# The norm of the recurrent mixer's memory, moved from the fifth FFN's beginning to the fourth's

## The reference

```python
def rms_norm(x, g):
    y = x * lax.rsqrt(jnp.mean(x * x, axis=-1, keepdims=True) + NORM_EPS)
    return y * g

# first block, second layer
x = ffn_step(x, ...)                               # third FFN
x = x + mx[5] * diff_attention(...)                # its last matrix is w_o
x = ffn_step(x, norm_g[1, 2], ...)                 # fourth FFN ("ffn", 3)
x = rms_norm(x, final_g)                           # final norm of the first block
# second block, first layer
x = x + 0.5 * swiglu_ffn(x, ffn_pre_norm[0], ...)  # fifth FFN ("ffn", 4)
u = rms_norm_2(x, mix_norm[0])
k, v = jnp.split(rms_norm_2(mem, mem_norm_g) @ w_kv, 2, axis=-1)   # memory's keys and values
...                                                # recurrent mixer and memory attention
```

## Time and profile before

| | |
|---|---|
| time, median of 3 runs | 2893.64 us (2890.03 to 2897.38) |
| the profiled execution | 2892.83 us, of which the span is 2891.2 us |
| TensorE's mean granted clock | 0.983 |
| TensorE, matmuls | busy 2770.5 us (96%) |
| VectorE | busy 2065.3 us (71%) |
| ScalarE | busy 1025.5 us (35%) |
| GpSimd | busy 81.5 us (3%) |

### The profile page before, as it was taken

One profiled execution on the slowest core, in us unless ns is written; L12 is line 12 of the kernel. 1 busy time (PEld: TensorE's weight loads), 2 busy tenths in 40 slices (PEclk: granted clock), 3 DMA queues, 4 the chain that ended last, 5 costly groups with the idle time before them and its releaser, 6 DMA issues.

```text
span 2891.2 us, 49358 instructions
## 1 busy us (share of the span) xinstructions
PE 2770.5 (96%) x19380; PEld 2447.1 (85%) x19380; DVE 2065.3 (71%) x3075; ACT 1025.5 (35%) x1158; POOL 81.5 (3%) x152
## 2 busy tenths in 40 slices
PE   6999999999999999999999899998999999998999
PEld 4888878888878888788799899887799989986999
DVE  6877778866777777776666766666767766665677
ACT  5222224222232222233344444452144434343433
POOL 1000000000000000000000000000000000000000
PEclk9999999999999999999999999999999999998999
DMA  8444441443334444322245344421044544443354
GB/s 328 160 147 180 172 154 66 161 151 131 131 117 160 146 181 170 112 95 74 84 175 189 131 174 174 180 88 60 3 166 175 202 125 174 185 164 66 117 186 177
DMA packets 68704, 421.42 MB, mean 146 GB/s; under 512 B 7672, under 2 KB 8824, under 8 KB 26592
## 3 DMA queue, kind: packets, MB, share of 16 engines
q1 hardware_dynamic: 48032, 341.26, 31.8%
q0 software_dynamic: 20576, 78.78, 8.4%
HBM read 418.94 MB, written 1.07 MB: 145 GB/s over the span
## 4 chain that ended last, share of the span: by engine, by line
PE 87%; DVE 7%; issue 3%; ACT 2%; DMA 1%; DVEq 0%; SPq 0%; ACTq 0%
PE ps_o L2133 11%; PE ps_o L2135 11%; PE ps_o L2134 11%; PE ps_g L2133 7%; PE ps_u L2133 7%; PE ps_u L2135 7%; PE ps_u L2134 7%; PE ps_g L2134 7%; PE ps_g L2135 7%; PE ps_g L2148 2%; DVE wlo L1191 1%; PE ps_o L2353 1%; ACT whi L706 1%; DMA wraw<-in_W 1%; DVE tsq L1244 1%
## 5 line engine op out<-in xcount | busy, mean ns | idle before, releaser
L706 ACT ACTIVATE whi<-wraw 128x2048 fp32r<-128x2048 f32 x323 | 616.1, 1911 | 788.0 <-PE ps_u L2135 382.8
L1191 DVE TENSOR_TENSOR wlo<-wraw,whi 128x2048 fp32r<-128x2048 f32 x323 | 731.3, 2286 | 160.5 <-ACT whi L706 160.3
L2133 PE MATMUL ps_o<-ah,wlo 128*128 128x256 f32 (+1 forms) x1408 | 462.6, 329 | 19.2 <-issue 15.4
L2133 PE MATMUL ps_g<-hh,wlo 128*128 128x256 f32 (+1 forms) x1464 | 463.3, 316 | 13.2 <-ACT tsq L821 7.4
L2133 PE MATMUL ps_u<-hh,wlo 128*128 128x256 f32 (+1 forms) x1464 | 462.0, 316 | 0.3 <-DVE wlo L1191 0.2
L2135 PE MATMUL ps_g<-hh,whi 128*128 128x256 f32 (+1 forms) x1464 | 462.1, 316 | 0.0
L2135 PE MATMUL ps_u<-hh,whi 128*128 128x256 f32 (+1 forms) x1464 | 462.0, 316 | 0.0
L2134 PE MATMUL ps_u<-hl,whi 128*128 128x256 f32 (+1 forms) x1464 | 461.8, 315 | 0.0
L2134 PE MATMUL ps_g<-hl,whi 128*128 128x256 f32 (+1 forms) x1464 | 461.8, 315 | 0.0
L2135 PE MATMUL ps_o<-ah,whi 128*128 128x256 f32 (+1 forms) x1408 | 454.0, 322 | 0.0
L2134 PE MATMUL ps_o<-al,whi 128*128 128x256 f32 (+1 forms) x1408 | 453.3, 322 | 0.0
(11 more groups left out here) (456 smaller groups left out, 3712.8 us busy)
## 6 DMA issues: line engine op xcount, KB each, us to landing
wraw<-in_W SPq DMA_DIRECT2D x324, 1024.0 KB, 4.8
scr<-in_ADA POOLq DMA_DIRECT2D x126, 512.0 KB, 3.8
scr<-bias_rows POOLq DMA_DIRECT2D x8, 384.0 KB, 8.5
x<-in_XT POOLq DMA_DIRECT2D x1, 2048.0 KB, 10.5
x<-in_MEMT POOLq DMA_DIRECT2D x2, 1024.0 KB, 6.1
cst<-in_CST POOLq DMA_DIRECT2D x1, 1511.5 KB, 7.0
cst<-in_CB POOLq DMA_DIRECT2D x1, 1024.0 KB, 6.6
scr<-in_PM POOLq DMA_DIRECT2D x1, 1024.0 KB, 5.0
```

What stands on the lines that cost most here:

```text
L706: nc.scalar.activation(whi[:, n % SLOTS, :], wraw[:, n % SLOTS, :], ACT.Copy).then_inc(w_hi, 1)
L1191: tt_(wlo[:, n % SLOTS, :], wraw[:, n % SLOTS, :], whi[:, n % SLOTS, :].bitcast(f32), sub).then_inc(w_lo, 1)
L2133: mm(out, a[1], b[0], start=first, stop=False)
```

## The change

The squares of the memory stand on ScalarE inside the norm ahead of the fourth FFN, behind its first square (`between`). On TensorE that norm has no `keep_clock` of its own; the memory's sums follow it, into a bank of `ps_o` that the fourth FFN's down tiles use later, and then two of the 128x512 matmuls. Root and conversions, reciprocal, products and low parts stand on ScalarE and VectorE between that norm and the fourth FFN. The final norm on TensorE takes its default of three 128x512 matmuls in place of none. The memory's second norm, for the last layer, keeps its place and its bank.

```diff
+        mem_sums = [ps_o[:, TILE0[FIRST["ffn", 3]] % BANKS, 0:NX], ps_u[:, 0, 0:NX]]
...
                     for d in range(0 if not squared else KT, KT):
                         square(src, N, ready, d)
+                        if d == 0 and between is not None:
+                            between()
...
             def memory_std(l):
                 act.wait_ge(me_sum, l + 1)
-                nc.scalar.activation(rstd[:, NX:NTOK], ps_u[:, 0, 0:NX], ACT.Sqrt, ...)
+                nc.scalar.activation(rstd[:, NX:NTOK], mem_sums[l], ACT.Sqrt, ...)
...
# ScalarE's list
-            norm(lambda d: x[:, d, :], NX, mod(1, 2), "split", after(FIRST["ffn", 3]), FIRST["ffn", 3])
+            norm(lambda d: x[:, d, :], NX, mod(1, 2), "split", after(FIRST["ffn", 3]), FIRST["ffn", 3], between=lambda: memory_squares(0))
+            memory_std(0)
+            memory_hi(0)
             ffn(3, NX)
-            memory_squares(0)
             norm(lambda d: x[:, d, :], NX, None, "final", after(FIRST["ffn", 4]), FIRST["ffn", 4])
-            memory_std(0)
             t_final = st["t"]
             norm(lambda d: x[:, d, :], NX, None, "split", lambda eng, d: eng.wait_ge(nm_t, t_final), FIRST["ffn", 4])
-            memory_hi(0)
             ffn(4, NX)
...
# VectorE's list
             norm(xs_, NX, A_mod(1, 2), B_mod(1, 2), "split")
+            memory_factor(0)
+            memory_norm(0)
             ffn(3, NX, gate(1, 2))
             norm(xs_, NX, gain("final_g"), None, "final")
-            memory_factor(0)
             dve.wait_ge(nm_t, st["t"])
             norm(xs_, NX, gain("ffn_pre_norm_2", 0), None, "split")
-            memory_norm(0)
             ffn(4, NX, half)
...
# TensorE's list
+            def memory_sums(l):
+                pe.wait_ge(me_sq, KT * (l + 1))
+                if l == 0:
+                    pe.wait_ge(o_free, TILE0[FIRST["ffn", 3]] + 1)
+                for d in range(KT):
+                    ins = mm(mem_sums[l], ones, mem_sq[d], start=d == 0, stop=d == KT - 1)
+                ins.then_inc(me_sum, 1)
             hh, hl, ah, al = narrow
-            norm(NX)
+            norm(NX, idle=0)
+            memory_sums(0)
+            keep_clock(2, BANK[3])
             ffn(3, NX)
-            norm(NX, False, idle=0)
-            memory_sums(0)
+            norm(NX, False)
             norm(NX)
             ffn(4, NX)
```

More of the change, by code:

```diff
@@ L710, in square, with norm @@
                 nc.scalar.activation(tsq[:, d * NTOK:d * NTOK + N], src(d)[:, 0:N], ACT.Square).then_inc(nm_sq, 1)
-            def norm(src, N, B, mode, ready, n, part=None, squared=False, again=False, memory=None, early=False, then=None, o=0, rows=range(KT)):
+            def norm(src, N, B, mode, ready, n, part=None, squared=False, again=False, memory=None, early=False, then=None, o=0, rows=range(KT), between=None):
                 k = st["k"]
@@ L789, in memory_std @@
                 act.wait_ge(me_sum, l + 1)
-                nc.scalar.activation(rstd[:, NX:NTOK], ps_u[:, 0, 0:NX], ACT.Sqrt, bias=C("eps", 1), scale=1.0 / D).then_inc(me_std, 1)
+                nc.scalar.activation(rstd[:, NX:NTOK], mem_sums[l], ACT.Sqrt, bias=C("eps", 1), scale=1.0 / D).then_inc(me_std, 1)
             def memory_hi(l):
@@ L2628, in _ @@
             diff_out()
-            hh, hl, ah, al = narrow
-            norm(NX)
-            ffn(3, NX)
             def memory_sums(l):
                 pe.wait_ge(me_sq, KT * (l + 1))
+                if l == 0:
+                    pe.wait_ge(o_free, TILE0[FIRST["ffn", 3]] + 1)
                 for d in range(KT):
-                    ins = mm(ps_u[:, 0, 0:NX], ones, mem_sq[d], start=d == 0, stop=d == KT - 1)
+                    ins = mm(mem_sums[l], ones, mem_sq[d], start=d == 0, stop=d == KT - 1)
                 ins.then_inc(me_sum, 1)
+            hh, hl, ah, al = narrow
+            norm(NX, idle=0)
+            memory_sums(0)
+            keep_clock(2, BANK[3])
+            ffn(3, NX)
             def memory_kv(l):
```

## The result

The changed kernel takes 2901.3 us (median of 15 runs, 2898.19 to 2909.07), the kernel before in the same measurement 2894.12 us (15 runs, 2889.71 to 2898.41). The ratio is 1.0029, with a 95% interval of 1.0021 to 1.0037: about 8 us slower, clear of noise, and on the bound of 0.3%. The forecast was 2902.6 us, +0.31%. The profiled execution is the slowest of the fifteen: 2909.07 us, span 2907.4.

What follows compares the result with a forecast made beforehand. TensorE, on 87% of the chain that ended last, was taken as the bound. Terms 6.9 - 0.1 + 0.8 + 1.5 = +9.1 us, rounded to +9.0, gave 2902.6 us (+0.31%); range 2896 to 2908 us.

Steps and rivals of the forecast that it cites:

- the bound of 0.3%: Line between same and slower at 2902.3 us, 8.7 us above 2893.64, about what a measurement can tell from no change.
- the sum's fixed terms: Restart in the fourth FFN 6.9 us later, including 2.1 us before the last projection tile; 0.1 us gained between FFNs.
- The relay: Norm ahead of the fourth FFN: eight memory squares delay ScalarE's square 1, so TensorE's second sum starts 2.1 us late.
- TensorE's longer list: Ahead of the fourth FFN: eight sums and two keep-busy matmuls replace three; an extra 1.0 us, hidden because ScalarE is later.
- The norm ahead of Silu: Rest of the memory norm precedes the fourth FFN's first activation: restart 6.9 us later, including 2.1 us from the squares.
- What comes back: Between fourth and fifth FFN: squares leave ScalarE, but VectorE's row 0 limits the gain to 0.1 us (bounds 0 and 0.15).
- Rival 2: Between the FFNs more comes back: row 0 earlier, low clock at 1644 gone; 2898.4 to 2900.8 us, chance 0.06.
- The clock: TensorE's clock falls after new waits: 0.8 us (0 or 1.6, even odds) before the last tile, 1.5 us at the restart.
- the long wait: TensorE's wait for Silu before the fourth FFN's loop grows from 1.4 to 5.2 us; lowered clock costs 0.7 to 3.

## Why the prediction was right

The time was right to 1.3 us and the sum's fixed terms to 0.1 us each. The first is finer than the measurement: the interval of the ratio is 6 to 11 us, and the difference of the medians was 7.2 us where 9.0 was forecast (the terms of the sum add up to 9.1). So that the total came so near is partly luck; that the fixed terms did isn't. Distances, before and after, in us:

| | before | forecast | after | also |
|---|---|---|---|---|
| first sum to root, clock high | 6.53 | +2.1 | | +2.18 (squares and sums alone) |
| the same, clock lowered behind the wait | | +3.7 | +3.77 | |
| root to restart | 16.89 | +4.8 | +4.83 | +4.84, +4.83, +4.83, +4.83 in four others |
| last pass to first sum of the final norm | 5.31 | -0.1 | -0.11 | -0.11 in the changed kernel's second profile |

*The relay.* Right: ScalarE has time for eight more squares, but a whole block stood ahead of something that TensorE wanted at once. Moving it behind row 6 took this wait away.

*TensorE's longer list.* Right: hidden, as long as the memory's norm is longer. The kernel without keep-busy matmuls has the same restart; the kernel with squares and sums alone shows the uncovered 0.84 us (1.0 forecast).

*The norm ahead of Silu.* Right, and the largest part. The table moved by itself gave 1.42 us; the table and the reciprocal ahead of the weight split together gave 2.85 us. The reciprocal wasn't moved alone.

*What comes back.* Right: 0.1 us. The 2.55 us of squares that left ScalarE's list between the FFNs had stood right ahead of a row that TensorE waited for, but VectorE delivered that row only 0.1 us before ScalarE came to it. Rival 2 falls: the wait ahead of 1644 grew as forecast (3.5 us), its end didn't move, and the low clock stayed.

*The clock.* The mechanism was right, and the size at the relay; the size at the long wait was too small, though inside the stated 0.7 to 3 us. Behind the relay's wait the clock fell in four of the profiles with that wait and not in two; where it fell it cost 3.77 - 2.18 = 1.6 us, as forecast for the case that it falls. Behind the long wait it cost 173.70 - 171.43 = 2.3 us, and 2.5 in the kernel with squares behind row 6 (172.31 against 169.83), where I had taken 1.5; the 171.43 us are those of the kernel with squares and sums alone, which had the same pass time and no low clock in that FFN. In the kernel with the table ahead, where the wait was 3.97 us, it cost 1.4 (171.23 against 169.83). In the changed kernel's profile a third fall, behind the wait ahead of the first sum of the final norm, cost another 1.6 us (8.18 us from that sum to the root, 6.58 before). The prediction had read this wait as one that doesn't lower the clock, from one profile. The second profile of the kernel before has 8.18 us there too, and so do, within 0.05 us, the two kernels with nothing but tables added; of the eight profiles with the change or parts of it, five had the fall and three hadn't. So this fall differs between executions and isn't the change's. The Trainium skill (TensorE: Matmul & The Clock Gate, "Terms") would count half of the time at the low clock; of the 5.1 us after the restart that is an estimate of 2.5 us, and 2.3 were lost.

*What was missing* is the pass time, and the clock in the rest of the kernel. The profiled execution's 16.2 us are, up to the fifth FFN: 2.6 that it brought with it, 2.2 + 4.8 - 0.1 of waits, 1.6 + 2.3 + 1.6 of clock, 1.6 of passes, less 0.2 in the sums at the low clock: 16.4, as read. Only the 6.9 us of waits were the same in every profile of the changed kernel. The fifteen times of the changed kernel lie in two heaps, and the granted clock on record goes with them: 0.980 to 0.982 for the eight up to 2901.3 us, 0.979 for six of the seven from 2904.7 us on (0.981 for the other). The change's cost as a whole was 7.2 and 10.3 us by the medians of the two measurements, 8.7 and 12.0 by the means. With the sizes that the profiles show, 6.9 of waits, two thirds of 1.6 and 2.3 to 2.5 us of clock, it is an estimate of 10.4 us. That the first fell on the bound of 0.3% is in the spread of the two.

## What to carry to other kernels

Before work is moved, find for each engine which instruction behind the new place is wanted first, and by whom; a block of eight cheap instructions cost 2.2 of its 2.5 us where it stood between two links of a relay, and nothing six instructions later. Cover belongs to a place: the same norm was free where its reciprocal had been done in an earlier gap, and cost 4.8 us where it had to be done in line. A short chain of waits that ends in an activation function's first use deserves attention of its own: a table load placed in a gap ahead of it took 1.2 to 1.6 us out of the chain in each of three FFNs, and 1.0 us in each of two more; in the second FFN the next wait took the gain back. So follow a gain to the next wait before it is counted.

## What the hardware showed that I hadn't expected

TensorE's matmul stream of one and the same loop ran in some FFNs of an execution with 16.80 us a pass and in others with 16.96, at a granted clock of 1.00 in both, constant within an FFN and different from one execution to the next. What sets it stays open. It and, more than it, the granted clock go with differences of 12 us between executions of one program (2889.11 to 2900.76 us in 26 of the kernel before on one chip). A pair of executions can't tell a change of 8 us, while a distance between two waits repeated to 0.1 us from profile to profile.
